# Six edits of order and of waits in a hybrid-mixer and mixture-of-experts layer

## The chip, the cores and the metric
The kernel runs as one program on one core of a Trainium2 chip. A core has a matrix engine (TensorE, PE in the profile), three engines for elementwise work (VectorE or DVE, ScalarE or ACT, GpSimd or POOL), and SyncE (SP), which here only issues DMAs. Each engine works through its own list of instructions in order and waits on semaphores that others raise. The metric is the device time of one execution in microseconds (us), the median over runs. Lower is better.

## The reference
Input `x` is 1024 tokens of 1024 features in float32. The layer is:

```
h   = LN_in(x)
mix = hybrid_mixer(h)      # one projection, 4 token mixers, sigmoid gates, output projection
h   = LN1(alpha*h + mix)
ffn = moe_ffn(h)           # sigmoid top-6 of 64 routed SwiGLU experts, plus one shared expert
h   = LN2(alpha*h + ffn)
```

The router scores each token against 64 experts, keeps 4 of 8 groups and then 6 experts. A routed expert takes its tokens' rows, computes `silu(x@wg) * (x@wu) @ wd`, scales by the token's weight and adds the rows into the sum. The shared expert does the same for all tokens without a router.

## The kernel before, in words
Everything is float32 on TensorE apart from small bf16 products of zeros and ones. The 1024 tokens are 8 tiles of 128. The order on each engine is written by hand, as the order of the calls; semaphores with counted values tie the engines together. Banks are the 8 PSUM accumulators (`bank[:, n, :]`). There are these stages:

- **Input norm and first projections** (`norm_in_and_project`). SyncE brings the tiles of `x`. VectorE takes a tile's statistics (`statistics(i)`: sums at L623, mean and variance at L626, epsilon at L628), ScalarE takes the root (`deviation(i)`, L565), VectorE the reciprocal and the shift (`normalize(i)`, L633 and L636), and ScalarE scales tiles 0 to 2 (L576). VectorE itself scales tile 3 (L640). TensorE then turns the four tiles, tile after tile (`turn_tiles`, L727), and the projections begin at L279.
- **Block products** (`block_part`, L776). Six 256-column weight slots are computed with a fast scheme of 7 half-size products in place of 8. For block n, ScalarE copies products 0, 2, 4 and 6 out of PSUM (L604), VectorE joins products 1, 3 and 5 (`join`, L688 to L693), GpSimd makes sums of weights (`mix_weights`, L494 to L499) and one sum of blocks (`cross(n)`, L505). The copy of product 6 of block n waits for `cross(n)`, and product 1 of block n+1 waits for that copy, as it writes the same bank. GpSimd also scales eight rows of h for later use and stores them (`keep_row(m)`, L518, L520, DMA at L522); VectorE's L706 waits for the last of them.
- **Token mixers**, about 200 to 919 us, which the change doesn't touch.
- **Merge** (`merge`). Eight pairs of products p (L2013) take branch after branch, again with 7 products each. VectorE joins (L2074) and weighs by the gates (L2089); ScalarE copies (L2032) and takes sigmoids; GpSimd adds into the result (L2135). `token_sums(b)` (L2061 to L2066) are four VectorE additions that prepare branch b's tokens; branch 1 is used by pairs 6 and 7 alone.
- **Output projection, LN1, router, shared expert** (`norm_and_route`). Per tile: `mix` (L2284), `norm`, `turn` (L2294, copied at L2558), `logits` (L2308), `count` (L2319), then the shared expert's `up` (L2332), `turn_hidden` (L2339), `down` (L2348). VectorE's `choose` picks experts, `placed` gives each token its place in the expert's list (it reads the counts and raises `pos`), `hidden` is L2443, `sum_base` is L2436. Near the end the routed experts' lists begin: `select` (L3102), `lists` on TensorE (L2773, into bank 0), `index` (L3107 reads bank 0, L3112, L3116, and 16 small writes at L3124), the gather of rows by GpSimd (L3140), and `turned` (L3154), which turns the gathered rows.
- **Experts.** A loop over the experts: `lists(b+3)`, `up(b)` (L3161), `down(b-1)` (L3177), `turn_hidden(b)` (L3169). Weights of 3 MB an expert come from memory into a ring of four slots. Then LN2.

Of the kernel before, what the change touches and what calls it, by code (L numbers as in the profile page):

```python
# [33 lines left out]
KT = D // P  # L34
NT = T // P
# [319 lines left out]
def norm_in_and_project(g):  # L355
# [75 lines left out]
    with nc.Block() as block:  # L431
# [41 lines left out]
        def _(pool):  # L473
# [28 lines left out]
            def cross(n):  # L502
                pool.wait_ge(copied, 4 * n + 3)
                pool.wait_ge(joined, 3 * n + 2)
                pool.tensor_tensor(kept(n, 4), kept(n, 4), kept(n, 3), ALU.add).then_inc(crossed, 1)  # L505
# [20 lines left out]
            keep_row(2)  # L526
            keep_row(3)
            mix_weights(2)
            keep_row(4)
            cross(1)  # L530
            keep_row(5)
            keep_row(6)
            mix_weights(3)
            keep_row(7)
            cross(2)
            mix_weights(4)
            for k in range(2):
                pool.wait_ge(h_kept[k], 16 * NT // 2)
# [78 lines left out]
        def _(dve):  # L617
# [33 lines left out]
            statistics(0)  # L651
            normalize(0)
            statistics(1)
            for i in range(2, 4):
                statistics(i)
                normalize(i - 1)
            dve.wait_ge(x_normed, 3)
            normalize(3)
            dve.wait_ge(gain_in, 32)
# [1234 lines left out]
def merge(g):  # L1894
# [161 lines left out]
    def vector(dve):  # L2056
        def token_sums(b):
            (b11, b12), (b21, b22) = right(b)
            t1, t2, t4 = right_sums(b)
            first = 4 * turn[b]  # L2060
            dve.tensor_tensor(t1, b12, b11, ALU.subtract).then_inc(s["tsum"], 1)  # L2061
            dve.wait_ge(s["tsum"], first + 1)
            dve.tensor_tensor(t2, b22, t1, ALU.subtract).then_inc(s["tsum"], 1)
            dve.tensor_tensor(b12, b22, b12, ALU.subtract).then_inc(s["tsum"], 1)
            dve.wait_ge(s["tsum"], first + 2)
            dve.tensor_tensor(t4, b21, t2, ALU.subtract).then_inc(s["tsum"], 1)  # L2066

        def join(p, e):
            r, i, c = ((1, 0, 1), (4, 2, 0), (5, 1, 1))[e]
            for x in range(2):  # L2070
                n = 2 * p + x
                dve.wait_ge(s["part"], 14 * p + 2 * r + x + 1)
                dve.wait_ge(s["copied"], 6 * p + 2 * (0, 2, 1)[e] + x + 1)
                dve.tensor_tensor(outs[x][i], outs[x][i], product_bank(n, c), ALU.add).then_inc(s["joined"], 1)  # L2074

        def weigh(p, e):
            i, out = ((0, 0), (3, 2), (1, 1), (2, None))[e]
            for x in range(2):
                n = 2 * p + x
                if n:  # L2080
                    dve.wait_ge(s["sig"], sigs(p, e, x))
                else:
                    dve.wait_ge(g.proj_read, projected)
                if e < 3:
                    dve.wait_ge(s["joined"], 6 * p + 2 * e + x + 1)
                else:
                    dve.wait_ge(s["part"], 14 * p + 12 + x + 1)
                other_side = outs[x][out] if e < 3 else product_bank(n, 0)
                dve.tensor_tensor(gates(n, i), gates(n, i), other_side, ALU.mult).then_inc(s["gated"], 1)  # L2089

        for b in (3, 2, 0):
            token_sums(b)
        for p in range(NP):
            join(p, 0)
            weigh(p, 0)
            if p == 2:
                dve.wait_ge(s["part"], 28)
                token_sums(1)
            join(p, 1)
            weigh(p, 1)  # L2100
            join(p, 2)
            weigh(p, 2)
            weigh(p, 3)
# [70 lines left out]
def norm_and_route(g, w, joint):  # L2174
# [9 lines left out]
    def h1T(m):  # L2184
        return merged[:, :, m * P:(m + 1) * P]
# [40 lines left out]
    flat2 = lambda a: bank[:, a:a + 2, :].rearrange("p b n -> p (b n)")  # L2226
    up_bank = [5, 5, 5, 5, 1, 3, 1, 5]

    def mix_bank(m):
        return 6 if m == 1 else 0  # L2230
    h_in = [sem(f"h_in{m}") for m in range(NT)]
# [43 lines left out]
    def tensor(pe, lists):  # L2275
# [22 lines left out]
        def logits(m):  # L2298
            pe.wait_ge(s["Tr"], m + 1)
            if m:  # L2300
                pe.wait_ge(s["lgr"], m)
            else:
                pe.wait_ge(s["wr"], 64)
            counted = m if m == NT - 1 else m + 2 - LAG
            if counted > 0:
                pe.wait_ge(s["pos"], counted)
            for k in range(KT):
                mm = pe.matmul(bank[:, 4, 0:NE], h1T(m)[:, k, :], wr[:, k, :], start=(k == 0), stop=(k == KT - 1))  # L2308
            mm.then_inc(s["lg"], 1)

        def count(m):
# [88 lines left out]
    def vector(dve, select, index, turned_first):  # L2400
# [133 lines left out]
        index(1)  # L2534
        select(2)
        sum_base(5)
        hidden(7)
        index(2)
        select(3)
        sum_base(6)  # L2540
        turned_first()
        first.last_sum = lambda: sum_base(NT - 1)

    def scalar(act):
# [14 lines left out]

        def score(m):  # L2560
            act.wait_ge(s["lg"], m + 1)
            act.activation(scores[:, m, :], bank[:, 4, 0:NE], ACT.Sigmoid).then_inc(s["lgr"], 1)

        def gate(m):
            act.wait_ge(s["gu"], m + 1)
# [107 lines left out]
def experts(g):  # L2673
# [62 lines left out]
    with nc.Block() as block:  # L2736
# [25 lines left out]
        def _(pe):  # L2762
# [5 lines left out]

            def lists(i, c):
                pe.wait_ge(s["q"], val(i, c) + 1)  # L2770
                wait(pe, s["idx"], val(i, c))
                for m in range(NT):
                    mm = pe.matmul(bank[:, 0, 0:6], w.q[:, m, :], values_of(g, m, expert(i, c)),  # L2773
                                   start=(m == 0), stop=(m == NT - 1))
                mm.then_inc(s["lst"], 1)
# [553 lines left out]
```

## Time and profile before

| | us |
|---|---|
| median of 3 runs | 2079.43 (2078.07 to 2079.71) |
| profiled execution | 2077.46 |
| its span, from first to last instruction | 2075.7 |
| PE busy | 1997.8 (96% of the span) |
| DVE busy | 1137.7 (55%) |
| POOL busy | 772.7 (37%) |
| ACT busy | 504.5 (24%) |
| DMA | 370.45 MB, mean 178 GB/s |

The page gives times of one execution; it lies 1.76 us above its span. Busy shares are averages over stages that differ. The chain that ended last says which engine the end waited for; a wait row says how long an engine stood before an instruction and who released it. A timeline row is: start, duration, engine, line, operation, output and inputs, count, and in brackets the idle time before it with its releaser. Neighbouring instructions of one line are merged into one row.

### The profile page before, as it was taken

Reading aid. Unit: us, or ns where it says so; the run is one execution under the profiler, and the core shown is the slowest. Engines: PE = TensorE matmul, PEld = TensorE weight load, DVE = VectorE, ACT = ScalarE, POOL = GpSimd, SP = SyncE. Lnnn points to the kernel's source line nnn. Section 1 sums busy time; section 2 is a strip of 40 time slices with the busy share of each in tenths; the row PEclk is TensorE's granted clock in tenths of the full one; section 3 lists DMA queues with packets and bytes.
Section 4 is the critical chain, followed back from the end, with each engine's and each line's share of the span. In section 5 each row is a group of like instructions: output and inputs, shape, how many; then the busy total and the mean of one; then the engine's idle time right before and its main releaser. Section 6 shows DMA issues by size and latency. Waiting matters only on the chain.

```text
span 2075.7 us, 23704 instructions
## 1 busy us (share of the span) xinstructions
PE 1997.8 (96%) x7237; PEld 1015.4 (49%) x7238; DVE 1137.7 (55%) x3065; ACT 504.5 (24%) x1102; POOL 772.7 (37%) x717
## 2 busy tenths in 40 slices
PE   7999999999999999999999999999999999999992
PEld 6444667575544444444445554444444444444440
DVE  6221546776622222335676656866666666666645
ACT  3111554453312222324432220011111111111113
POOL 1762005622122221215980002455455454455441
PEclk9999999999999999999999999999999999999996
DMA  5421000011132222144253006899999999999974
GB/s 146 129 89 41 21 21 21 22 47 46 43 125 79 73 81 76 55 123 168 101 206 145 31 36 251 310 330 357 352 352 359 356 354 359 347 352 358 349 256 171
DMA packets 129639, 370.45 MB, mean 178 GB/s; under 512 B 33712, under 2 KB 65668, under 8 KB 103832
## 3 DMA queue, kind: packets, MB, share of 16 engines
q1 hardware_dynamic: 103960, 314.83, 40.3%
q0 software_dynamic: 23520, 54.61, 11.0%
q8 instruction: 44, 0.72, 0.1%
q10 hardware_dynamic: 2080, 0.01, 0.1%
q14 instruction: 35, 0.29, 0.0%
HBM read 320.57 MB, written 68.17 MB: 187 GB/s over the span
## 4 chain that ended last, share of the span: by engine, by line
PE 44%; POOL 4%; DVE 4%; issue 3%; DMA 1%; ACT 0%; SPq 0%; DVEq 0%; POOLq 0%
PE banks L3161 22%; PE banks L3177 10%; PE banks L2284 4%; POOL arena L2135 2%; PE banks L2332 2%; PE banks L279 1%; PE banks L2348 1%; PE banks L2773 1%; PE banks L3169 1%; PE banks L2308 1%; DVE arena L3154 0%; DMA arena<-in_w_router_dram 0%; DVE arena L3237 0%; DVE index L3124 0%; POOL arena L2117 0%
## 5 line engine op out<-in xcount | busy, mean ns | idle before, releaser
L3161 PE MATMUL banks<-arena 128*128 128x512 f32 x1056 | 471.1, 599 | 5.7 <-DVE arena L3154 3.5
L3140 POOL DMA_INDIRECT arena<-h_rows,index x268 | 279.3, 1042 | 152.6 <-DVE index L3124 73.5
L3161 PEld LDWEIGHTS banks<-arena 128*128 128x128 f32 x1056 | 196.1, 191 | 230.0 <-issue 226.1
L1719 PE MATMUL banks<-arena 128*128 128x512 f32 x672 | 299.0, 594 | 1.8 <-ACT arena L323 1.8
L3177 PE MATMUL banks<-arena 128*128 128x512 f32 x528 | 237.6, 592 | 1.3 <-ACT arena L2976 0.8
L3154 DVE STREAM_TRANSPOSE arena<-arena 128x1024 f32<-128x1024 f32 x66 | 133.9, 2029 | 136.7 <-PE banks L3161 136.7
L3148 POOL DMA_INDIRECT sums<-arena,row_to x66 | 107.1, 1622 | 269.6 <-DMA sums<-arena,row_to 244.2
L279 PE MATMUL banks<-arena 128*128 128x512 f32 x416 | 191.8, 598 | 2.2 <-PEq L108 2.2
L1719 PEld LDWEIGHTS banks<-arena 128*128 128x128 f32 x672 | 123.1, 190 | 136.4 <-issue 133.9
L3124 DVE TENSOR_SCALAR index<-row 32x1 uint32<-32x1 f32 x1072 | 155.3, 145 | 17.1
L3177 PEld LDWEIGHTS banks<-arena 128*128 128x128 f32 x528 | 100.2, 190 | 127.0 <-issue 125.3
L776 PE MATMUL banks<-arena 128*128 128x512 f32 x336 | 145.1, 593 | 2.7 <-ACT arena L604 2.5
L285 PE MATMUL banks<-arena 128*128 128x256 f32 (+1 forms) x640 | 143.8, 366 | 0.0
L2971 ACT ACTIVATE arena<-banks 128x256 f32<-128x256 f32 x65 | 25.0, 384 | 434.4 <-PE banks L3161 434.4
L2013 PE MATMUL banks<-arena 128*128 128x512 f32 x280 | 120.9, 593 | 1.7 <-DVE arena L2074 1.6
L285 PEld LDWEIGHTS banks<-arena 128*128 128x128 f32 x640 | 105.4, 190 | 19.9 <-issue 10.8
L2284 PE MATMUL banks<-arena 128*128 128x512 f32 x256 | 112.7, 594 | 1.5 <-POOL arena L2135 1.4
L279 PEld LDWEIGHTS banks<-arena 128*128 128x128 f32 x416 | 74.3, 190 | 74.2 <-issue 73.0
L776 PEld LDWEIGHTS banks<-arena 128*128 128x128 f32 x336 | 63.4, 190 | 83.0 <-issue 78.0
L2983 ACT ACTIVATE arena<-banks,weight 128x512 f32<-128x512 f32 x64 | 44.0, 688 | 203.6 <-PE banks L3177 203.6
L2884 DVE TENSOR_SCALAR arena<-banks,weight 128x512 f32<-128x512 f32 x64 | 48.1, 751 | 75.7 <-PE banks L3177 75.7
L2013 PEld LDWEIGHTS banks<-arena 128*128 128x128 f32 x280 | 53.0, 190 | 69.3 <-issue 64.0
(400 smaller groups left out, 2429.6 us busy)
## 6 DMA issues: line engine op xcount, KB each, us to landing
arena<-in_w_exp_gate_dram SPq DMA_DIRECT2D x66, 1024.0 KB, 8.0
arena<-in_w_exp_up_dram SPq DMA_DIRECT2D x66, 1024.0 KB, 10.2
arena<-in_w_exp_down_dram SPq DMA_DIRECT2D x66, 1024.0 KB, 17.2
arena<-in_w_in_dram SPq DMA_DIRECT2D x26, 1024.0 KB, 5.3
gates<-arena SPq DMA_DIRECT2D x60, 256.0 KB, 2.0
arena<-gates SPq DMA_DIRECT2D x15, 1024.0 KB, 7.6
arena<-h_rows,index POOLq DMA_INDIRECT x268, 8.0
arena<-in_x_dram SPq DMA_DIRECT2D x8, 512.0 KB, 6.4
```

Of the source, the lines that this page charges most:

```text
L279: mm = pe.matmul(bank[0:width], w[:, q, col:col + width], g.hT[:, q, at * HALF:(at + 1) * HALF], start=(q == 0), stop=(q == KT - 1))
L285: mm = pe.matmul(bank[:, m * width:(m + 1) * width], g.hT[:, k, (at + m) * P:(at + m + 1) * P], w[:, k, col:col + width], start=(k == 0), ...
L776: mm = pe.matmul(block_bank(n, b), left[:, k, :], right[:, k, :], start=(alone and k == 0), stop=(k == 3), skip_group_check=True)
L1719: mm = pe.matmul(gate_bank(n, b), left[:, k, :], right[:, k, :], start=(alone and k == 0), stop=(k == 3), skip_group_check=True)
L2013: mm = pe.matmul(product_bank(n, c), lhs[:, k, :], rhs[:, k, :], start=(alone and k == 0), stop=(k == deep[b] - 1), skip_group_check=True)
L2284: mm = pe.matmul(bank[:, mix_bank(m) + h, :], merged[:, k, m * P:(m + 1) * P], wout[k][:, h * HALF:(h + 1) * HALF], start=(k == first), st ...
L3124: ins = dve.tensor_scalar(g.index[32 * b:32 * b + 32, k, q:q + 1], g.row[32 * q:32 * q + 32, k, :], 4.0, float(b), ALU.mult, ALU.add)
L3140: return pool.indirect_dma_start(w.x[k][:, 256 * q:256 * (q + 1)], None, rows, bass.IndirectOffsetOnAxis(ap=g.index[:, k, q:q + 1], axis=0 ...
L3148: return pool.indirect_dma_start(g.sums, bass.IndirectOffsetOnAxis(ap=g.row_to[:, b:b + 1], axis=0), w.y[k], None, bounds_check=last, oob_ ...
L3154: return dve.transpose(w.xT.rearrange("p k (q n) -> p q k n", q=4), w.x[k].rearrange("p (q n k) -> p q k n", q=4, k=KT))
L3161: mm = pe.matmul(g.bank[:, 2, :].rearrange("p (a f) -> p a f", a=2), xT[:, k, :], wgu[:, :, k, :], start=(k == 0), stop=(k == KT - 1))
L3177: mm = pe.matmul(g.bank[:, 4 + h, :], hidT[:, k, :], wdn[:, k, h * HALF:(h + 1) * HALF], start=(k == 0), stop=(k == 1))
```

## The change
Six edits, none of which adds or removes an instruction on the arrays:

1. GpSimd: `cross(1)` stands ahead of `keep_row(4)`, and `cross(2)` ahead of `keep_row(7)`.
2. VectorE: `normalize(1)` and `normalize(2)` stand right behind their own tile's statistics, no longer behind the next tile's.
3. Merge: `token_sums(1)` is made in pair 3 and no longer in pair 2.
4. Router: the last tile's logits go to bank 2, and TensorE doesn't wait for `pos` there.
5. VectorE, end of the router stage: `turned_first` (the turn of the first expert's rows) and `select(3)` stand ahead of `hidden(7)`; they stood behind `sum_base(6)` and `index(2)`.
6. TensorE's `lists` waits until VectorE has read bank 0 (`list`), no longer for the 16 index writes behind that (`idx`).

```diff
@@ gpsimd, block products
             mix_weights(2)
+            cross(1)
             keep_row(4)
-            cross(1)
             keep_row(5)
             keep_row(6)
             mix_weights(3)
+            cross(2)
             keep_row(7)
-            cross(2)
@@ vector, input norm
             statistics(1)
-            for i in range(2, 4):
-                statistics(i)
-                normalize(i - 1)
+            normalize(1)
+            statistics(2)
+            normalize(2)
+            statistics(3)
@@ vector, merge
-            if p == 2:
+            if p == 3:
                 dve.wait_ge(s["part"], 28)
                 token_sums(1)
@@ router
+    def logit_bank(m):
+        return 2 if m == NT - 1 else 4
...
-            counted = m if m == NT - 1 else m + 2 - LAG
-            if counted > 0:
-                pe.wait_ge(s["pos"], counted)
+            if m < NT - 1 and m + 2 > LAG:
+                pe.wait_ge(s["pos"], m + 2 - LAG)
...
-                mm = pe.matmul(bank[:, 4, 0:NE], h1T(m)[:, k, :], wr[:, k, :], start=(k == 0), stop=(k == KT - 1))
+                mm = pe.matmul(bank[:, logit_bank(m), 0:NE], h1T(m)[:, k, :], wr[:, k, :], start=(k == 0), stop=(k == KT - 1))
@@ vector, end of the router stage
         sum_base(5)
+        turned_first()
+        select(3)
         hidden(7)
         index(2)
-        select(3)
         sum_base(6)
-        turned_first()
@@ tensor, lists
-                wait(pe, s["idx"], val(i, c))
+                wait(pe, s["list"], val(i, c))
```

GpSimd, first of the two moved sums: L505 is `cross(1)`, L518 to L522 are `keep_row(4)`, L497 and L499 end `mix_weights(2)`; a minus is a row of before, a plus one of now.

```order
 L497 TENSOR_TENSOR arena<-arena 128x512
 L499 TENSOR_TENSOR arena<-arena 128x512 [waits k_wsum]
-L518 TENSOR_TENSOR arena<-arena 128x1024 [waits h_kept0,k_wsum]
-L520 TENSOR_TENSOR arena<-arena 128x1024 [waits h_made]
-L522 DMA h_rows<-arena 128x1024 [waits h_made]
-L505 TENSOR_TENSOR arena<-arena 128x512 [waits k_joined,k_copied]
+L505 TENSOR_TENSOR arena<-arena 128x512 [waits k_joined,k_copied,k_wsum]
+L518 TENSOR_TENSOR arena<-arena 128x1024 [waits h_kept0]
+L520 TENSOR_TENSOR arena<-arena 128x1024 [waits h_made]
+L522 DMA h_rows<-arena 128x1024 [waits h_made]
```

One addition moved past two additions and a DMA issue; `cross(2)` moved past `keep_row(7)` in the same way.

VectorE at the end of the router stage, before: from `select(2)` (L3102) to the turn of the first expert's rows (L3154).

```order
L3102 TENSOR_TENSOR arena<-iota,arena 128x1024
L2436 SCALAR_TENSOR_TENSOR arena<-arena,banks 128x1024
L2443 TENSOR_TENSOR arena<-arena,banks 128x256
L3107 TENSOR_REDUCE list<-banks 128x2
L3112 TENSOR_SCALAR flag<-list,pad_row 128x1
L3116 SCALAR_TENSOR_TENSOR row<-list,flag 128x1
L3124 TENSOR_SCALAR index<-row 32x1 x16
L3102 TENSOR_TENSOR arena<-iota,arena 128x1024
L2436 SCALAR_TENSOR_TENSOR arena<-arena,banks 128x1024
L3154 STREAM_TRANSPOSE arena<-arena 128x4x8x32
```

The same place now; each line number from the router on is 3 higher (L3157 is the turn, L3105 `select`, L2446 `hidden`, L2439 `sum_base`).

```order
L3105 TENSOR_TENSOR arena<-iota,arena 128x1024
L2439 SCALAR_TENSOR_TENSOR arena<-arena,banks 128x1024
L3157 STREAM_TRANSPOSE arena<-arena 128x4x8x32
L3105 TENSOR_TENSOR arena<-iota,arena 128x1024
L2446 TENSOR_TENSOR arena<-arena,banks 128x256
L3110 TENSOR_REDUCE list<-banks 128x2
L3115 TENSOR_SCALAR flag<-list,pad_row 128x1
L3119 SCALAR_TENSOR_TENSOR row<-list,flag 128x1
L3127 TENSOR_SCALAR index<-row 32x1 x16
L2439 SCALAR_TENSOR_TENSOR arena<-arena,banks 128x1024
```

The turn and `select(3)` moved ahead of `hidden(7)` and the six rows behind it; nothing else moved.

## Rows read from the trace of the kernel before

**Rows 1.** The page, part 4: chain that ended last, by engine.

```profile
PE 44%; POOL 4%; DVE 4%; issue 3%; DMA 1%; ACT 0%; SPq 0%; DVEq 0%; POOLq 0%
```

**Rows 2.** Waits of PE: line, releaser, us in total, times, longest.

```profile
PE banks L3161 <- DVE arena L3154: 3.5, 2, 2.7
PE banks L776 <- ACT arena L604: 2.5, 1, 2.5
...
PE banks L2308 <- DVE arena L2499: 1.8, 1, 1.8
...
PE banks L2013 <- DVE arena L2074: 1.6, 1, 1.6
```

**Rows 3.** Timelines of ACT, DVE and PE's weight loads, 0 to 20 us.

```profile
9.15 0.20 ACT L565 ACTIVATE rstd<-rstd 128x1 f32<-128x1 f32 x1 [0.97 <-DVE rstd L628]
12.93 1.24 ACT L576 ACTIVATE arena<-arena,shift,rstd 128x1024 f32<-128x1024 f32 x1 [0.56 <-DVE shift L636]
...
14.57 0.81 DVE L640 TENSOR_SCALAR arena<-arena,mv,rstd 128x1024 f32<-128x1024 f32 x1
...
15.78 1.66 PEld L727 LDWEIGHTS banks<-ident,arena 128*128 128x128 f32 x8
```

**Rows 4.** Timelines of PE, DVE and POOL, 86 to 136 us.

```profile
86.62 17.43 PE L776 MATMUL banks<-arena 128*128 128x512 f32 x40 [0.22 <-DVE arena L688]
...
127.23 1.23 DVE L706 TENSOR_SCALAR arena<-arena 128x2048 f32<-128x2048 f32 x1 [2.52 <-POOL arena L520]
...
134.35 0.69 DVE L688 TENSOR_TENSOR arena<-arena,banks 128x512 f32<-128x512 f32 x1 [1.19 <-PE banks L776]
...
104.54 1.27 POOL L505 TENSOR_TENSOR arena<-arena 128x512 f32<-128x512 f32 x1
...
128.60 1.27 POOL L505 TENSOR_TENSOR arena<-arena 128x512 f32<-128x512 f32 x1
```

**Rows 5.** Timeline of DVE in the merge.

```profile
919.19 0.69 DVE L2061 TENSOR_TENSOR arena<-arena 128x512 f32<-128x512 f32 x1 [6.66 <-PEq L108]
...
976.57 1.76 DVE L2061 TENSOR_TENSOR arena<-arena 128x512 f32<-128x512 f32 x1
...
982.21 1.27 DVE L2074 TENSOR_TENSOR arena<-arena,banks 128x512 f32<-128x512 f32 x2
...
1000.41 0.69 DVE L2074 TENSOR_TENSOR arena<-arena,banks 128x512 f32<-128x512 f32 x1 [4.79 <-PE banks L2013]
```

**Rows 6.** Timeline of ACT and DVE around the last logits.

```profile
1237.23 1.02 ACT L2558 ACTIVATE arena<-banks 128x1024 f32<-128x1024 f32 x1 [0.70 <-PE banks L2294]
```

**Rows 7.** Timelines of PE, DVE and POOL, 1255 to 1330 us.

```profile
1284.27 0.34 PE L2773 MATMUL banks<-arena 128*128 128x6 bf16 x8
...
1287.99 0.38 PE L2339 MATMUL banks<-ident,arena 128*128 128x128 f32 x2
...
1292.74 9.38 PE L3161 MATMUL banks<-arena 128*128 128x512 f32 x16 [2.69 <-DVE arena L3154]
...
1305.82 7.11 PE L3161 MATMUL banks<-arena 128*128 128x512 f32 x16
...
1278.74 1.22 DVE L2436 SCALAR_TENSOR_TENSOR arena<-arena,banks 128x1024 f32<-128x1024 f32 x1
1284.89 0.42 DVE L2443 TENSOR_TENSOR arena<-arena,banks 128x256 f32<-128x256 f32 x1 [4.93 <-ACT arena L2568]
...
1290.68 2.00 DVE L3154 STREAM_TRANSPOSE arena<-arena 128x1024 f32<-128x1024 f32 x1
...
1271.97 1.01 POOL L3140 DMA_INDIRECT arena<-h_rows,index  x1 [0.30 <-issue]
```

**Rows 8.** Line L3140, 1265 to 1300 us: from issue to landing.

```profile
DMA to landing us min/median/max: 2.3/3.0/3.5
```

**Rows 9.** Stretches by engine: us, PE, PEld, DVE, ACT, POOL busy, granted clock, DMA share, GB/s.

```profile
1293.00:1295.00 2.00, 2.00 (x3) 0.90 (x4) 1.81 (x13) 0.00 (x0) 1.14 (x2) 0.50 0.93 252
...
1345.00:1900.00 555.00, 553.00 (x1703) 262.07 (x1702) 367.10 (x1271) 67.32 (x150) 284.13 (x250) 1.00 1.00 352
```

More of the change, by code:

```diff
@@ L2561, in score @@
             act.wait_ge(s["lg"], m + 1)
-            act.activation(scores[:, m, :], bank[:, 4, 0:NE], ACT.Sigmoid).then_inc(s["lgr"], 1)
+            act.activation(scores[:, m, :], bank[:, logit_bank(m), 0:NE], ACT.Sigmoid).then_inc(s["lgr"], 1)
         def gate(m):
```

## The prediction, made before the result was known
> **What bounds the kernel now.** I read the chain that ended last first: it lies on PE for the largest part, with short pieces on POOL and DVE [rows 1]. So I asked where PE stands idle, in its list of waits, and then read the timelines of the engines around each gap. Only two of PE's 1056 expert products of L3161 waited for the turn of rows, and 3.5 us in all [rows 2]. From 1345 to 1900 us PE is busy 553.0 of 555.0 us at full clock [rows 9]. What TensorE gains ahead of that stretch is therefore carried to the end, unless the weights for the experts come too late. Each edit is aimed at one gap of PE; the question for each is whether the gap closes and what is late next.
>
> **The sum is made against the profiled execution, 2077.46 us.** The median of the runs is 2079.43, so 1.97 is added at the end.
>
> **Edit 2, input norm.** The root of tile 1 is done at 9.15 + 0.20 = 9.35 [rows 3]. Now the reciprocal follows at once. I take 0.4 us from the root's end to the scaling's start, and get tile 1 scaled from 9.77 to 11.01. Tile 2's statistics start some 0.6 us later than before, since they stand behind the normalising. They take 1.71, the root and the reciprocal 0.66, so ScalarE scales tile 2 from 12.02 in place of 12.93 [rows 3]. Tile 3 is done by VectorE from 14.08 in place of 14.57 [rows 3], since its statistics now come last. It is ready at 14.89. PE turned tile 3 from 15.78 [rows 3], as it was still busy with tile 2. With tile 2 ready at 13.26, its eight transposes (1.58) end at 14.88, so tile 3 starts at 14.93. Gain 0.85. From below: if VectorE's last step alone counts, 0.49. If each of the three round trips to ScalarE is slower by the 0.27 us that the fastest takes, the gain is 0. I take 0.85.
>
> **Edit 1, the block sums.** PE's products of L776 run from 86.62 for 17.43 us, to 104.05, and then wait 2.5 us for ScalarE's copy [rows 2, 4]. That copy waits for `cross(1)`, which ran from 104.54 to 105.81, behind `keep_row(4)` [rows 4]. The row of 86.62 holds five products of 3.43; the last is product 0 of block 2, so product 6 of block 1 ended at 100.6. `cross(1)` now starts where `keep_row(4)` started, 5.65 earlier (98.9), and ends at 100.15. The copy of product 6 follows at 100.7 and is done at 101.3, before PE needs the bank at 104.05. The gap of 2.5 goes. Would it come back at `cross(2)`? Before, it ended at 128.60 + 1.27 = 129.87, and its copy at 130.57, when PE got to the next product at about 130.6: just in time. With PE 2.5 earlier that would cost the whole gain, so the second move is what keeps it. There `cross(2)` runs 6.2 earlier, done at 123.6, and PE needs its copy at 128.1. Behind it `keep_row(7)` is 1.27 later, and VectorE's L706 waits for it: 128.5 in place of 127.23 [rows 4]. VectorE's queue behind that is L706, L708, L709 and then the join of block 3, which starts at 134.3 and is done at 135.0. PE needs it at 137.46 - 2.5 = 134.96. So VectorE is late by 0.05. Gain 2.45. Bounds: 2.5 above; below 1.2, if these three operations also slow each other down by the 1.27 of one addition.
>
> **Edit 3, the merge.** VectorE's four token additions stand from 976.57 to 982.21 ahead of the join on which PE waited 1.6 (1.55 in its timeline) [rows 2, 5]. Without them this join can run from 978.9, when its product ends (PE's products here take 0.86 each), and PE needs it at 981.4: the gap goes. In pair 3 the products are twice as deep, and VectorE idles 4.79 us ahead of the same join (1000.41) [rows 5]. The additions cost 4 x 0.69 = 2.8 when nothing else runs and 5.6 next to GpSimd [rows 5]. So the join there is late by at most 0.9. PE takes product 6 of that pair about 3 us later, so nothing is lost. Gain 1.55. Bounds: 0, if POOL's additions, which the last `mix` waits for, are delayed as much as PE is ahead; 1.55.
>
> The additions alone take 0.69, next to GpSimd up to 1.76 [rows 5]. The Trainium skill (SBUF — State Buffer, Who interferes with whom) says more than "slower": a VectorE operation with two SBUF inputs and a GpSimd operation that reads SBUF exclude each other, and the later one blocks until the other ends. It speaks against this move, as in pair 3 GpSimd adds into the result without a pause. By that rule each of the four additions could wait for one whole GpSimd addition of about 1.4 us: 8.4 us, the join 3.6 late, PE 0.6 late, and the edit would be worth 0.95 in place of 1.55.
>
> **Edit 4, the last logits.** PE waited 1.8 for VectorE's `placed(6)` (L2499) [rows 2]. Without it the next conditions are the copy of tile 7 to SBUF, which ended at 1238.25 [rows 6], and PE's own work before it, which ends where the gap began. The gap goes. Next in line is `count(7)`, behind the 7.0 us of `up(4)`; VectorE's choice of experts moves by 1.15 only, being held by `sum_base(2)`, and still comes some 0.7 us ahead of PE. Gain 1.75; 1.15 if VectorE sets the pace.
>
> **Edits 5 and 6, the first expert.** In the old times of this stretch: the first gather was issued by 1271.97 + 1.01 = 1272.98 and lands 3.0 us later (3.5 at most) [rows 7, 8]. Its rows were turned only at 1290.68 [rows 7], because five things stand ahead of it. VectorE was idle 4.93 us up to 1284.89 [rows 7]. Now the turn starts at the end of `sum_base(5)`, 1278.74 + 1.22 = 1279.96, and is done at 1282.0. `select(3)` waits for `lists(2)`, done at 1284.61 [rows 7], and ends at 1285.9. Queued behind it is `hidden(7)`, to 1286.3, 0.95 later than before. For it PE waits at 1287.99 [rows 7], so 1.7 us are left. `index(2)` reads bank 0 at 1286.4; `lists(3)` needs just that, by edit 6. With the old wait it would stand until `index(2)` ends at 1289.35, 1 us late. So PE goes from 1287.99 through the turn of hidden and `lists(3)` (0.2 each) to `up(0)` at 1288.40, in place of 1292.74 [rows 7]: 4.34. The gather of expert 2 starts 0.95 later, but is used 20 us later. `sum_base(6)` ends at 1290.6; `down(7)` needs it at 1295.5.
>
> `up(0)` itself took 9.38, the next one 7.11 [rows 7]. In 1293 to 1295 us the granted clock was 0.50, that is 1.2 GHz, after PE had stood nearly idle since 1288.4; from 1345 on it is 1.00, 2.4 GHz [rows 9]. Without the idle time there is no reason for the fall: 2.27 more. Together 6.6. Bounds: 0, if a wait of the new queue takes the old one's place; 6.6.
>
> That the clock is at 0.50 in one stretch is a row of one execution. The Trainium skill (TensorE: Matmul & The Clock Gate, What's actually happening) warns that the moment of a switch varies from run to run. By that, other executions would lose less or more at this place, and the 2.27 would be worth between 0 and about 3. The sum would be lower by up to 2.3.
>
> Behind `up(0)` VectorE's queue is as before, and so are the 1.5 us that PE loses there to the overflow tables.
>
> **Sum.** 0.85 + 2.45 + 1.55 + 1.75 + 6.6 = 13.2. 2077.46 - 13.2 = 2064.3; with 1.97, 2066.2.
>
> **The rivals.**
> - *The new queue of the first expert waits itself.* VectorE holds `hidden(7)`, `index(2)` and `sum_base(6)` behind a turn that waits for a DMA and a `select` that waits for TensorE. If these cost what they save, 6.6 stays: 2066.2 + 6.6 = 2072.8. For it: only 1.7 us are left ahead of PE at 1287.99. Against: the gather's landing at 1276 leaves 4 us. Chance 0.08.
> - *The weights hold the experts.* DMA is busy at 1.00 from 1345 to 1900 at 352 GB/s [rows 9]. If the experts' pace is that of the DMA, an earlier start ends in a wait for weights, and only the tail remains: about 2079, no change. Against: PE is busy 553.0 of 555.0 there and shows no wait for a DMA; loads are asked for by PE's own progress. Chance 0.05.
> - *The gains of the merge and the clock fail, the rest holds:* 2066.2 + 1.55 + 2.27 = 2070. Chance 0.10.
> - *Slower.* The turn of the first rows now stands ahead of everything VectorE owes to TensorE. If the first gather lands late, each us is one us lost: `up(0)` would start about 4.4 us behind the landing (turn 2.0, `select` 1.2, `hidden` 0.4, TensorE's steps 0.8). It decides from a landing at 1292.7 + 2.3 + 6.6 - 4.4 = 1297, where all other gains are used up; at 1302 the time would be 2084. For it: in 1250 to 1260 the DMA queues are full of expert weights. Against: it landed within 3.5 us of its issue [rows 8]. Chance 0.03.
>
> **How the numbers follow.** Forecast 0.74; the four rivals 0.08, 0.05, 0.10, 0.03. The measurement tells a change from none from about 0.2%, 4.2 us. All cases but the second and the last give more than that: faster 0.92, same 0.05, slower 0.03. The forecast's own range is 2064 (all terms at their upper bounds and the runs' own spread of 1.6) to 2069 (the small terms at their lower bounds). I take in the third rival and part of the first: 2063.5 to 2071.
>
> **What would show it.** PE's list of waits should lack L776 for ScalarE, L2013 for VectorE, and the waits of the last logits and of L3161's first product. The first `up` of the experts should take 7.1 us at clock 1.00. The wait for L2135's last additions (1.4) should stay, as should the gap of 1.5 in front of L3169 (L3172 now). It is wrong if a new wait of VectorE at `select(3)` moves `turn_hidden(7)`, if POOL's wait ahead of the last `mix` grows by what the merge gained, or if PE waits for weights within the loop.

## The result: 2063.07 us, faster by 0.8%, and beyond the range

| | before | after |
|---|---|---|
| median, us | 2079.57 (2078.07 to 2084.37) | 2063.07 (2061.21 to 2065.85) |
| profiled execution, us | 2077.46 | 2065.85 |
| span, us | 2075.7 | 2064.1 |
| mean granted clock | 0.989 | 0.989 |

The ratio is 0.9918, with a 95% interval of 0.9898 to 0.9938. The gain is 16.5 us, and 12.9 to 21.2 by the interval. The sum had 13.2, and the forecast of 2066.2 us was 3.1 too high. Its range ended at 2063.5, so the time is 0.4 us outside it. These four executions alone don't tell 13.2 from 16.5, and that the time lies outside by 0.4 us is within the draw of four: together with the five of the repeat below, the median of the changed kernel is 2063.82, inside the range. The profiled execution of the changed kernel was the longest of its four.

In the code after, a line number of before stands 1 higher from L655 on, and 3 or 4 higher from the router on. PE's waits in the changed kernel: line, releaser, us in total, times, longest.

```profile
PE banks L728 <- ACT arena L576: 9.2, 3, 8.2
PE banks L279 <- PEq L108: 2.2, 1, 2.2
PE banks L2776 <- issue: 1.9, 1, 1.9
PE banks L3172 <- DVE arena L2880: 1.8, 2, 1.5
...
PE banks L3164 <- DVE arena L3157: 0.7, 1, 0.7
```

Of the four waits of [rows 2], those for the block sum, the last logits and the token sums are gone, and the one for turned rows is down from 3.5 to 0.7 us. None of the new queues has a wait of its own here. The largest single gaps left behind the input are the two that no edit touches: 2.2 us at the change of stage (L279) and 1.9 us where registers are loaded (L2776).

Timelines of the changed kernel, in the places of [rows 3], [rows 4] and [rows 5]:

```profile
11.82 1.24 ACT L576 ACTIVATE arena<-arena,shift,rstd 128x1024 f32<-128x1024 f32 x1 [0.42 <-DVE shift L636]
...
13.96 0.81 DVE L640 TENSOR_SCALAR arena<-arena,mv,rstd 128x1024 f32<-128x1024 f32 x1
...
97.78 1.26 POOL L505 TENSOR_TENSOR arena<-arena 128x512 f32<-128x512 f32 x1
...
99.58 0.60 ACT L604 ACTIVATE arena<-banks 128x512 f32<-128x512 f32 x1 [6.27 <-PE banks L777]
...
978.15 1.27 DVE L2075 TENSOR_TENSOR arena<-arena,banks 128x512 f32<-128x512 f32 x2
...
989.74 1.76 DVE L2062 TENSOR_TENSOR arena<-arena 128x512 f32<-128x512 f32 x1
...
995.64 1.38 DVE L2075 TENSOR_TENSOR arena<-arena,banks 128x512 f32<-128x512 f32 x2
```

Tile 2 is scaled from 11.82 (forecast 12.02, before 12.93) and tile 3 from 13.96 (forecast 14.08). The block sum runs at 97.78, and ScalarE's copy waits for PE's product alone. VectorE's join in the merge runs at 978.15, and the token sums stand at 989.74, where PE has no wait.

The first expert, in the place of [rows 7]:

```profile
1272.44 2.02 DVE L3157 STREAM_TRANSPOSE arena<-arena 128x1024 f32<-128x1024 f32 x1
...
1280.55 0.38 PE L2342 MATMUL banks<-ident,arena 128*128 128x128 f32 x2
1280.77 0.34 PE L2776 MATMUL banks<-arena 128*128 128x6 bf16 x8
...
1280.97 7.11 PE L3164 MATMUL banks<-arena 128*128 128x512 f32 x16
```

The rows of the first expert are turned at 1274.5, 6.5 us ahead of PE's use of them. `lists(3)` and `up(0)` follow the turn of the hidden rows without a pause, and `up(0)` takes 7.11 in place of 9.38. The window of [rows 9] is as it was, so the weights don't hold the experts:

```profile
1345.00:1900.00 555.00, 552.96 (x1705) 261.85 (x1704) 364.31 (x1250) 67.18 (x150) 281.71 (x249) 1.00 1.00 353
```

**Where the time came from, by the two profiled executions.** The start of the same PE work, after less before, changes at each edit. These are differences of starts in the two timelines.

| stretch | term of the sum | in the profiles |
|---|---|---|
| input norm | 0.85 | 1.11 |
| block sums | 2.45 | 2.57 |
| token sums | 1.55 | 1.75 |
| last logits | 1.75 | 1.93 |
| first expert, start of `up(0)` | 4.34 | 4.40 |
| `up(0)`, its length | 2.27 | 2.27 |
| sum | 13.2 | 14.03 |

From 1301.96 (now 1287.92) PE leads by 14.04. Shifts at places that no edit touches cancel: 0.28 won in front of L1719 near 573, 0.34 lost around L2284 and L2294 between 1078 and 1093. So every term is right within 0.3, and 16.5 - 14.0 = 2.5 us is not in any of them. (A fall of the clock in each of the two, shown below, cancels: one at 307 in before, one at 913 in after.) The rest of the two profiles gives it no place: behind this point the changed kernel loses 2.4 again, and the spans differ by 11.6 only. 1.7 of the 2.4 are lost at one place, by the same thing that turned out to be missing from the sum. These are windows of the changed kernel, and under them one of before:

```profile
914.00:917.00 3.00, 3.00 (x4) 1.12 (x4) 2.93 (x6) 0.78 (x1) 0.00 (x0) 0.50 0.73 232
1952.00:1954.00 2.00, 2.00 (x4) 0.71 (x3) 1.83 (x14) 0.00 (x0) 0.82 (x1) 0.50 1.03 356
```

```profile
308.00:310.00 2.00, 2.00 (x6) 0.47 (x4) 0.00 (x0) 0.00 (x0) 0.00 (x0) 0.50 0.00 0
```

The column ahead of the last two is the granted clock: 0.50, 1.2 GHz, while PE is busy without a pause. Each such fall costs 1.7 us: by that the same PE work starts later behind it (1.68, 1.70 and 1.69 for these three). I had counted one, that of `up(0)`. The profile of before has a second at 307 us, and that of after has two at places where before has none. That the mean clock is the same in both is no evidence: PE's idle end is in it too, which began 15 us earlier in after.

### The profile page after: what moved, and what is told of

The parts are those of the page before. It is cut to its first block, busy times and chain, and to the rows that moved or that the text cites. A ratio compares the mean times of both kernels' runs of the same rounds, so it can differ in the third digit from the quotient of the medians.

```text
span 2064.1 us, 23702 instructions
## 1 busy us (share of the span) xinstructions
PE 1995.9 (97%) x7237; PEld 1014.8 (49%) x7238; DVE 1138.1 (55%) x3065; ACT 504.3 (24%) x1102; POOL 774.3 (38%) x717
## 4 chain that ended last, share of the span: by engine, by line
PE 46%; POOL 3%; DVE 2%; issue 2%; DMA 1%; ACT 0%; SPq 0%; DVEq 0%; POOLq 0%
PE banks L3164 22%; PE banks L3180 10%; PE banks L2288 4%; PE banks L2335 3%; POOL arena L2136 2%; PE banks L2014 2%; PE banks L279 1%; PE banks L2351 1%; PE banks L2776 1%; PE banks L3172 1%; PE banks L2311 1%; DMA arena<-in_w_router_dram 0%; DVE arena L3240 0%; DVE arena L3157 0%; PE banks L2298 0%
## 5 line engine op out<-in xcount | busy, mean ns | idle before, releaser
L3157 DVE STREAM_TRANSPOSE arena<-arena 128x1024 f32<-128x1024 f32 x66 | 133.9, 2028 | 134.3 <-PE banks L3164 134.3
L279 PE MATMUL banks<-arena 128*128 128x512 f32 x416 | 193.5, 602 | 2.2 <-PEq L108 2.2
L279 PEld LDWEIGHTS banks<-arena 128*128 128x128 f32 x416 | 74.9, 192 | 75.4 <-issue 74.1
```

The costliest lines, as they stand in the source:

```text
L279: mm = pe.matmul(bank[0:width], w[:, q, col:col + width], g.hT[:, q, at * HALF:(at + 1) * HALF], start=(q == 0), stop=(q == KT - 1))
L3157: return dve.transpose(w.xT.rearrange("p k (q n) -> p q k n", q=4), w.x[k].rearrange("p (q n k) -> p q k n", q=4, k=KT))
```

## The experiments

The first eight undo or keep single edits. They were run to check the terms. What they told beyond that is in the granted clock along each of their profiles.

**The change once more.** No edit.

> The changed kernel itself, once more. In the two profiled executions TensorE's path became 13.5 us shorter between its falls to half clock; each fall of 3.4 us at 0.50 costs 1.7 us, and the two executions had them at different places (307 and 1290 us before; 913 and 1951 us after). Theory A: the falls outside the gap at 1290 come by chance and about as often in either kernel, so the forecast of 13.2 us was right and the 16.5 us between the medians of four runs each were a lucky draw: the median gain here is 12 to 15 us, and the places of the falls are other ones again. Theory B: the closed gaps also took away places at which the clock falls, so that falls are rarer now: the gain is again 15 to 18 us, and the changed kernel's lowest time lies further below its forecast than the old kernel's lowest does.

2064.39 us (2062.22 to 2065.75), ratio 0.9922 (0.9909 to 0.9935). Its profiled execution took 2062.22 and has no fall at all up to PE's idle end. At the two places where the first profile had one, it reads:

```profile
914.00:920.00 6.00, 6.00 (x15) 2.65 (x15) 5.90 (x10) 0.89 (x1) 1.20 (x1) 1.00 0.84 315
1950.00:1957.00 7.00, 7.00 (x18) 3.09 (x17) 4.80 (x22) 0.38 (x1) 2.46 (x3) 1.00 0.99 376
```

The gaps ahead of these places were the same (2.2 and 2.1 us). So a fall is a matter of the execution, and one profile shows only one draw. The gain of 15.6 here is 13.5 to 18.9 by the interval: a little above the 13.2 of the sum. It favours theory B and doesn't exclude theory A's 15.

**First expert undone.** The queue of VectorE as before, `lists` waits for `idx` again.

```diff
-        turned_first()
-        select(3)
         hidden(7)
         index(2)
+        select(3)
         sum_base(6)
+        turned_first()
...
-                wait(pe, s["list"], val(i, c))
+                wait(pe, s["idx"], val(i, c))
```

> The changed kernel with edits 5 and 6 undone (the first rows turned behind sum_base(6), the lists waiting for the index writes). By the prediction this costs 4.34 us of waits ahead of the first expert's products and 2.27 us of half clock within them: 6.6 us against the changed kernel, with 9.4 us for the first up in place of 7.1. Rival: the clock fall there is chance too, then the first up takes 7.1 us and the cost is 4.3 us.

2073.08 us (2070.2 to 2074.84), ratio 0.996 (0.9947 to 0.9973): 8.7 above the change, where the sum had 6.6. The gaps of 1.3 and 2.7 us are back, and `up(0)` has its fall again, of 3.4 us: it takes 8.55 in place of the 9.4 expected. The profile has three more falls, at 305, 916 and 1961. That at 305 is at the place of the one at 307 in before, behind two gaps of 0.9 and 0.8 us.

**First expert alone**, the same lines put into the kernel before.

> The kernel before with edits 5 and 6 alone. If the gains add up, 6.6 us faster than before (theory A), all of it between the last logits and the first expert. If the falls of the clock hang on the other gaps of TensorE as well (theory B), this kernel still has them all and shows falls outside the first expert as often as the old one, so less than 7 us of the 16.5.

2074.32 us (2069.51 to 2075.24), ratio 0.9968 (0.9955 to 0.998): 5.7 below before. Together with the run ahead of it the two edits are worth 5.7 to 8.7, around the 6.6 of the sum. This profile has a fall that before did not have, right behind the open gap of the block sum, which ends at 106.9:

```profile
107.00:110.00 3.00, 3.00 (x4) 1.26 (x5) 0.00 (x0) 0.29 (x1) 2.92 (x2) 0.50 0.00 0
```

**The wait of `lists` undone**, the turn left early.

```diff
-                wait(pe, s["list"], val(i, c))
+                wait(pe, s["idx"], val(i, c))
```

> The changed kernel with edit 6 undone alone: lists waits for the 16 index writes again. By the prediction lists(3) then stands until index(2) ends, 1.0 us later (1289.35 against 1288.2 in the old times), and nothing else moves: 1.0 us slower than the changed kernel, none at the other experts. Rival: the reordering of VectorE makes the wait harmless or adds the clock's fall: 0, or 2.7 us.

2066.46 us (2064.46 to 2067.78), 2.1 above the change by the medians. The profile has the wait for `index(2)` with 1.0 us, as the prediction said it would be with the old semaphore. The rest is 0.9 us of waits for weights and a fall at 914.

**Second block sum, token sums, last logits, input norm: each undone alone.**

```diff
-            cross(2)
             keep_row(7)
+            cross(2)
```

> The changed kernel with cross(2) behind keep_row(7) again, cross(1) still ahead. By the prediction cross(2) is then done at the old 129.9 us (less the 1.1 that the input norm gained), while TensorE arrives 2.5 earlier, so the whole gain of edit 1 is lost at block 3: a new wait of 2.5 us at L777 behind ScalarE, 2.5 us slower than the changed kernel in the profile. Rival: cross(1) alone keeps the gain: 0. If gaps are where the clock falls, the time may be 1.7 more in some executions, with the fall just behind the gap.

```diff
-            if p == 3:
+            if p == 2:
                 dve.wait_ge(s["part"], 28)
```

> The changed kernel with token_sums(1) in pair 2 again: a wait of 1.55 us at L2014 near 976 us, 1.55 us slower in TensorE's path. Rival (GpSimd's additions bound the end of the merge): the wait ahead of the last mix shrinks by as much and the cost is 0 to 1.

```diff
-        return 2 if m == NT - 1 else 4
+        return 4
...
-            if m < NT - 1 and m + 2 > LAG:
-                pe.wait_ge(s["pos"], m + 2 - LAG)
+            counted = m if m == NT - 1 else m + 2 - LAG
+            if counted > 0:
+                pe.wait_ge(s["pos"], counted)
```

> The changed kernel with the last logits in bank 4 and the wait for pos: a wait of 1.77 us at L2310, 1.75 slower in TensorE's path; nothing later moves. Rival: VectorE's choose sets the pace behind it, then 1.1.

```diff
-            normalize(1)
-            statistics(2)
-            normalize(2)
-            statistics(3)
+            for i in range(2, 4):
+                statistics(i)
+                normalize(i - 1)
```

> The changed kernel with the old order of the input norm. The prediction had 0.85 us, the two profiles showed 1.11 at the first projection. 1.1 slower in TensorE's path at the first projection and still 1.1 at 200 us; in the timed runs that is within their spread of 2 us. Rival: VectorE's and ScalarE's later work in that stage absorbs it: 0 at 200 us.

| undone | median, us | ratio (95%) | above the change | gap back in the profile | falls in the profile |
|---|---|---|---|---|---|
| `cross(2)` | 2069.23 | 0.9945 (0.9927 to 0.9964) | 4.8 | 2.5 | 130, 918, 1956 |
| token sums | 2065.39 | 0.9935 (0.9916 to 0.9953) | 1.0 | 1.5 | none |
| last logits | 2069.01 | 0.9951 (0.9936 to 0.9966) | 4.6 | 1.8 | 914, 1238, 1955 |
| input norm | 2066.63 | 0.9937 (0.992 to 0.9955) | 2.2 | 1.1 | 916 |

Each gap comes back with the size of its term, `cross(2)` too: the second move does keep the first one's gain. But the times lie further off: the excess over the gap is 2.3, -0.5, 2.8 and 1.1, with an uncertainty of about 2 us each. Two of these profiles have a fall just behind the reopened gap, at 130 and at 1238. So far, then: falls of the clock stand behind gaps of PE, at the same few places, in some executions. That was theory B. Against it stood chance (A), and that the register loads at L2776 bring the fall (C).

**Fourteen gaps more.** The expert loop, in which PE has no gap, showed no fall in any profile. Here each of its 14 turns begins with five register loads.

```diff
+            def idle_gap():
+                pe.wait_ge(s["tabled"], 1)
+                for _ in range(5):
+                    rest_count(pe)
...
             def step(i, c):
+                if not isinstance(i, int) and c == 0:
+                    idle_gap()
                 if has(i, c, 3):
                     lists(i, c + 3)
```

> The changed kernel with one idle gap more in each of the 14 turns of the expert loop (1.3 to 1.9 ms), where it had none and TensorE's clock never fell in nine profiles: five loads of a register ahead of lists(i, 3), as they stand once, ahead of L2776, where they left PE idle for 1.9 us. Nothing is added to the matmuls. Theory B (the clock falls to 1.2 GHz only behind a place where PE stood idle, in some executions at each place; one fall costs 1.7 us): the 14 gaps cost 14 x 1.9 = 26.6 us, and behind them the profile shows falls, as often as behind the one gap at 1950 us (4 of 9 profiles), some 6 of 14, 10 us more: about 2064 + 26.6 + 10 = 2101 us. Rival A (the falls have nothing to do with gaps): no fall in the loop, 2091 us.

2147.26 us, ratio 1.0326 (1.0309 to 1.0342). The waits, then two gaps of the timeline, then windows over the fall behind the first of these gaps, the stretch after it, and the next fall:

```profile
PE banks L2776 <- issue: 48.5, 15, 8.3
```

```profile
1381.77 0.39 PE L3179 MATMUL banks<-ident,arena 128*128 128x128 f32 x2
1385.23 1.07 PE L2776 MATMUL banks<-arena 128*128 x8 [3.08 <-issue]
...
1435.34 1.07 PE L2776 MATMUL banks<-arena 128*128 x8 [2.99 <-issue]
```

```profile
1385.00:1391.00 6.00, 5.63 (x14) 2.84 (x15) 4.08 (x20) 0.00 (x0) 2.12 (x2) 0.50 1.02 407
1391.00:1434.00 43.00, 41.33 (x124) 19.25 (x122) 25.06 (x80) 5.39 (x12) 21.69 (x19) 1.00 0.87 302
1436.00:1442.00 6.00, 5.86 (x11) 2.65 (x11) 4.08 (x20) 0.00 (x0) 2.17 (x2) 0.50 1.01 378
```

The expectation had 2101 us and some 6 falls in 14; both were far too low. The gaps became 3.0 us, not 1.9 (the first one 8.3): ahead of L2776 there are three register loads in the changed kernel, not five, so five take longer. Behind all 14 the clock fell, and nowhere between them, where PE is busy without a pause (from 1432.3 on the second window lies in the next gap). The falls take some 3.4 us (4 of them), 6.8 us (9) or more (1). PE lost 48.5 us in gaps where it had 1.9, and the time rose by 83 us. The other 36 us, 2.6 for each gap, are the clock's. In the profile one turn of the loop takes 44.30 us in the changed kernel and 50.06 here, on average: 3.0 of gap and 2.8 more.

**The same loads with matmuls between them.**

```diff
+                for n in range(5):
+                    if n < 4:
+                        pe.matmul(bank[:, 1, 0:256], g.ident[:], expert_weights(g, 3)[1][:, 0, 0:256],
+                                  start=True, stop=True)
+                    rest_count(pe)
```

> The same 14 x 5 register loads, with four matmuls of 128x256 that nobody reads between them, so that PE isn't idle for 1.9 us at a stretch. Theory B: no falls in the loop; if the loads run beside the matmuls, 14 x 1.9 = 26.6 us over the changed kernel, 2091 us, and if they wait for each other 14 x 1.7 = 24 us more, 2115 us; in both cases without falls. Rival A: as many falls as in the kernel with bare gaps. Rival C (it isn't the idle time but the register loads that bring the fall): as many falls as with bare gaps too.

2116.73 us, ratio 1.0184 (1.0167 to 1.0201): 31 us less than with bare gaps, though PE has more to do. One turn takes 47.72 us, 2.3 less than with bare gaps. What was left of a gap was 0.9 us, and behind 13 of the 14 the clock stayed at 1.00:

```profile
1377.64 2.26 PE L2805 MATMUL banks<-arena,ident 128*128 128x256 f32 x8
1380.84 1.08 PE L2776 MATMUL banks<-arena 128*128 x8 [0.94 <-issue]
```

```profile
1380.00:1386.00 6.00, 5.01 (x17) 2.58 (x18) 3.50 (x20) 0.00 (x0) 1.61 (x1) 1.00 1.01 414
1345.00:1900.00 555.00, 542.66 (x1678) 259.21 (x1675) 340.78 (x1174) 63.13 (x141) 276.84 (x234) 1.00 0.94 331
```

From the end of the transposes to L2776 it is 2.8 us here and 3.1 with bare gaps: the matmuls (L2805) ran while the loads ran, and did not make the stretch longer. The 2115 us that the expectation gave for loads and matmuls that wait for each other was thus met by luck: the five loads by themselves take 3.0 us, not 1.9. The 31 us are the clock's alone.

The one fall, at 1329, stands at the first turn, where PE waited 4.2 us for the table. So it is the idle time, not the loads (C) and not chance (A).

**The kernel before, with its gaps filled.** No wait is shortened. PE runs matmuls that nobody reads while it waits: 2.1 us of them at 104, 1.3 at 981, 1.3 at 1241, 0.9 and 2.1 around 1290.

```diff
+                if n == 2 and r == 1:
+                    for wide in (512, 512, 256):
+                        pe.matmul(bank[:, 4, 0:wide], a11[:, 0, :], tok[0][0][:, 0, 0:wide], start=True, stop=True,
+                                  skip_group_check=True)
...
+                if isinstance(i, int) and i == 0 and c == 0:
+                    fill(512, 512, 256)
                 up(i, c)
```

> The kernel before with every wait that the change removes left as it is, but PE kept at work in it by matmuls that nobody reads: 2.1 us of them at 104 us, 1.3 us at 981, 1.3 us at 1241, 0.9 us at 1288 and 2.1 us at 1290. Theory B: behind these gaps, where they are open, the profiles so far show falls in 1 of 2 (104), 0 of 3 (981), 1 of 3 (1241), 2 of 2 (1290) cases, and the gap at 126 in 1 of 3 when it is open; filled they show none. No wait is shorter, yet the time is 1.7 us lower for each fall: (0.5 + 0.33 + 1) x 1.7 = 3.1 us, 2077 us against 2080.2 us, and no fall at 107, 1241 or 1290 in the profile. Rival A (the 3 us that the change gained beyond my sum are somewhere in the waits themselves): within 0.5 us of the kernel before, and a fall near 1290 again.

2075.36 us in 11 runs (2074.3 to 2077.7) against 2079.97, ratio 0.9976 (0.9967 to 0.9986). The clock alone is thus worth 4.6 us of the kernel before by the medians (2.9 to 6.9 by the interval). The expectation had 3.1. Its profile has one fall, at 917, where nothing was filled. The first expert, and the windows over the places at 1241 and 1290:

```profile
1289.99 0.35 PE L2785 MATMUL banks<-arena 128*128 128x6 bf16 x8 [0.46 <-DVE arena L3124]
1290.20 2.40 PE L2813 MATMUL banks<-arena,ident 128*128 128x512 f32 x6
1293.05 7.13 PE L3183 MATMUL banks<-arena 128*128 128x512 f32 x16 [0.46 <-DVE arena L3176]
```

```profile
1241.00:1246.00 5.00, 4.54 (x31) 3.21 (x27) 3.54 (x15) 2.49 (x4) 0.00 (x0) 1.00 0.19 74
1290.00:1298.00 8.00, 7.54 (x26) 3.55 (x27) 6.96 (x22) 0.00 (x0) 5.02 (x5) 1.00 0.86 314
```

`up(0)` starts at 1293.05, no earlier than before (1292.74), and takes 7.13 where it took 9.38. L2813 is the filling.

**The register loads of the changed kernel, filled.**

```diff
+                for k in range(AHEAD + 1):
+                    pe.matmul(bank[:, 1, 0:256], g.ident[:], expert_weights(g, 3)[1][:, 0, 0:256],
+                              start=True, stop=True)
+                    picked.append(chosen_expert(pe, k))
```

> The changed kernel with matmuls of 128x256 that nobody reads between the register loads ahead of the last experts, where PE stood idle for 1.9 us at 1948 us and the clock fell behind it in 4 of 9 profiles. Theory B: no fall at 1951, so 4/9 x 1.7 = 0.8 us less than the changed kernel, 2063.0 us, if the matmuls run beside the loads. Rival A: 2063.8 us, or up to 1.7 us more if each load waits for the matmul ahead of it.

2064.56 us (2063.03 to 2067.12), ratio 0.9932 (0.9918 to 0.9947): no gain over the change that could be told. In its profile there is no fall at 1951, but 7 of the 11 profiles with the bare gap have none either. The stretch from the last transpose to L2776 is 2.0 us, as with the bare gap (1.9 and 2.1 in the two profiles of the change): the 1.0 us of matmuls lies within the time of the loads, and 1.1 is left as a gap.

**The clock of every execution.** Each execution has its span and its mean granted clock. (1 - clock) x span is the full-speed time that the clock withheld. 17 to 20 us of it fall in PE's idle end by the profiles and cost nothing; the rest is falls. The clock is given to 0.001, 2 us, so only means are of use.

| kernel | executions | median, us | withheld, mean, us |
|---|---|---|---|
| before | 35 | 2080.0 | 24.1 |
| before, gaps filled | 11 | 2075.36 | 19.8 |
| changed | 9 | 2063.82 | 18.6 |
| first expert undone | 5 | 2073.08 | 22.4 |
| `cross(2)` undone | 4 | 2069.23 | 21.7 |
| token sums undone | 4 | 2065.39 | 18.6 |
| last logits undone | 6 | 2069.01 | 22.1 |
| input norm undone | 4 | 2066.63 | 21.2 |

Filling the gaps gave back 4.3 us of clock and 4.6 us of time. The change gave back 5.5 us of clock (3.7 to 7.1, 95%, by resampling the executions), where the sum had 2.27; the medians differ by 16.2 us (14.5 to 18.7), so that more than 13.2 was gained is settled by all of them together. Among the undone edits the order is that of the excess over the gap: 3.8 of clock for 4.3 us of time (first expert), 3.1 for 2.3, 0.0 for -0.5, 3.5 for 2.8, 2.6 for 1.1. Among the 35 executions of before, time and withheld clock go together with a correlation of 0.77.

## Why the prediction was right in its steps and wrong in its time

**The six edits.** Each did what its step said, in place and within 0.3 us: the norm 1.11 (0.85), the block sums 2.57 (2.45), the token sums 1.75 (1.55), the logits 1.93 (1.75), the first expert 4.40 (4.34). None of the bounds "a new wait takes its place" came true in the profile of the change. The rivals fall with them: the new queue has no wait of its own (2072.8), the weights hold nothing up (2079), the merge gave its gain (2070), the first gather was there, turned and all, 6.5 us ahead (2084).

**The step that failed** is the clock's, the "2.27 more" of edits 5 and 6 that stood for all of the clock. It was read from one execution, and only where it showed behind a gap that I was looking at. The medians of the kernel before carry more. At the gaps that the change closes, the profiles with the gap open showed a fall in 1 of 2 (at 104 us), 0 of 3 (981), 1 of 3 (1241) and 2 of 2 (1290). Filled, they showed none in the one profile, and the kernel was 4.6 us faster with every wait in place. The clocks of all executions say the same: 5.5 us less withheld than before, part of it in the gaps themselves. With 4.6 for the clock and the 11.76 that the five rows of waits in the table add up to (14.03 - 2.27), the sum is 16.4, and 16.5 was measured. So the term was 2.3 too small, and the waits together 0.8. That `up(0)` itself gave 2.27 to the digit is the match of one draw: with the first expert undone its fall cost 1.4 (8.55 - 7.11).

**The offset and the range.** The 1.97 us from the profiled execution to the median were treated as something that both kernels have. They were in part those falls, and went with the gaps: the profiled execution withheld 22.8 us of clock, the mean of 35 is 24.1. The low end of 2063.5 left 2.7 us below the forecast, for "all terms at their upper bounds" and a spread of 1.6 of the runs. The bounds of the edits lie 0.05 above their terms in all, which gives 2064.5; the rest of the way had no term. In the bounds of the edits the clock's term ended at its full 2.27, so nothing in the range stood for falls at the other gaps. That other executions may differ was weighed for one place only, as a risk to the 2.27. The Trainium skill (TensorE: Matmul & The Clock Gate, What's actually happening) says that the moment of a switch varies from run to run. The two profiles of the same kernel show more than that: there are two falls in one and none in the other. So of every gap that an edit closes one has to ask what it costs in other executions.

**VectorE beside GpSimd**, which was weighed against edit 3, did not decide there: in pair 3 the four additions took 5.9 us (989.74 to 995.64), near the 5.6 of the sum and not 8.4, and PE had no wait. Undoing the edit brought the gap of 1.5 back and cost 1.0. But the same contention showed where the sum had VectorE "late by 0.05". Timelines of the run with the logits undone, and of the repeated change:

```profile
128.72 2.47 DVE L709 TENSOR_SCALAR arena<-arena 128x2048 f32<-128x2048 f32 x1
128.82 1.27 POOL L494 TENSOR_TENSOR arena<-arena 128x512 f32<-128x512 f32 x1
...
135.13 10.14 PE L777 MATMUL banks<-arena 128*128 128x512 f32 x23 [1.20 <-DVE arena L689]
```

```profile
128.37 1.23 DVE L709 TENSOR_SCALAR arena<-arena 128x2048 f32<-128x2048 f32 x1
128.51 2.21 POOL L494 TENSOR_TENSOR arena<-arena 128x512 f32<-128x512 f32 x1
```

In the first, GpSimd's addition keeps its 1.27 and VectorE's operation takes twice its time; in the second it is the other way round. The join is late by 1.2 us in one and not in the other, though the program is the same up to there. It was late in three of the profiles with both sums moved (first expert undone, logits undone, fourteen gaps). The 1.2 that I had put as the lower end of edit 1 is thus real, in part of the executions.

**What stays open.** The falls of an execution that was not profiled can't be counted or placed; only its mean clock is known. Why a fall came behind the gap at 911 (2.2 us) in 7 of 14 profiles and behind that at 1949 (1.6 to 2.1 us) in 4 of 11, and not in the others, wasn't settled. The single undone edits add up to more than the whole: 8.7 + 4.8 + 1.0 + 4.6 + 2.2 = 21.3 against 16. With some 2 us of uncertainty each this may be chance, and no run here separates it. Two of the five profiles (first expert, logits) also have the join that is 1.2 us late at 134. That the excess is the clock for the most part follows from the clocks of the executions, that all of it is doesn't: what one closed gap outside the first expert is worth in clock is not measured one by one.

## What to carry to other kernels

When an edit closes an idle gap of PE, price the gap and the clock behind it as two terms, and read the second from several profiled executions, since one shows a draw. If the clock falls behind a gap in some of them, the expected loss belongs in the sum, and its absence in the range's far end. A wait that can't be removed can be covered with matmuls that nobody reads, if they run while PE would wait: that alone was worth 4.6 us here, for five gaps of 1.3 to 2.7 us. The length of a gap counts: single gaps of up to 1.6 us brought no fall here.

## What the runs showed of the hardware

- The granted clock has the two values 0.50 and 1.00 in all 14 profiles. How often it fell behind a gap of PE goes with the gap's length, between the input and PE's idle end:

| gap, us | falls |
|---|---|
| 1.0 to 1.6, alone | 0 of 50 |
| 1.7 to 2.1 | 5 of 13 |
| 2.2 | 7 of 14 |
| 2.5 to 2.7 (two with one of 1.3 just ahead) | 4 of 5 |
| 3.0 | 13 of 13 |

Each length stands at a few places of the kernel only, so length and place are told apart by the loop alone, where the same places had 3.0 us (13 of 13) and 0.9 us (0 of 13).

- Shorter gaps are not always harmless: behind the pair of 0.9 and 0.8 us near 305 the clock fell in 2 of 14 profiles. Behind the 13 gaps of 0.9 us with matmuls ahead (the filled loop) it never did.
- A fall of 3.4 us in which PE is busy costs 1.7 us of PE's time. Behind the 3.0 us gaps most took 6.8 us, and gap and fall together cost 5.6 us for each: nearly twice the gap.
- Register loads on PE's queue ran beside the matmuls issued ahead of them: with 2.3 us of matmuls between five loads the stretch took 2.8 us (bare 3.1), and with 1.0 us between three it took 2.0 us (bare 1.9 and 2.1). A load takes about 0.6 us.
- Two operations of VectorE and GpSimd that start within 0.2 us of each other: the one of the two that loses takes 2.2 to 2.5 us in place of 1.2, and which one that is depends on the execution.
